# Row projections that close their token tiles over one last weight chunk, and half columns ahead of transposes 2 and 3, in a two-layer decoder trunk

## The reference

```
m = even_mixer(x, w_qkv_ab, w_o_ab, cos, sin)     # layer 0;  odd_mixer(...) in layer 1
x = layer_norm(ALPHA * x + m, ln_mix_g, ln_mix_b)
f = conv_ffn(x, w_up, conv_w, conv_b, w_down)      # (silu(g) * val) @ w_down, g and val convolved
x = layer_norm(ALPHA * x + f, ln_ffn_g, ln_ffn_b)
```

## Time and profile before

| what | us |
|---|---|
| median of 3 runs (1303.65 to 1305.03) | 1305.0 |
| span of the profiled execution | 1303.8 |
| TensorE busy (matmul) | 1251.3 (96%) |
| VectorE busy | 661.0 (51%) |
| GpSimd busy | 558.9 (43%) |
| ScalarE busy | 497.5 (38%) |
| TensorE's mean granted clock over the span, share of full speed | 0.991 |

### The profile page before, as it was taken

One profiled execution on the slowest core, in us unless ns is written; L12 is line 12 of the kernel. 1 busy time (PEld: TensorE's weight loads), 2 busy tenths in 40 slices (PEclk: granted clock), 3 DMA queues, 4 the chain that ended last, 5 costly groups with the idle time before them and its releaser, 6 DMA issues.

```text
span 1303.8 us, 16570 instructions
## 1 busy us (share of the span) xinstructions
PE 1251.3 (96%) x6032; PEld 1022.0 (78%) x6032; DVE 661.0 (51%) x1043; ACT 497.5 (38%) x717; POOL 558.9 (43%) x248
## 2 busy tenths in 40 slices
PE   7999999998999999999989999989899999999996
PEld 7877777688888888888868777768788888888885
DVE  3056656527766666632281255661766666663226
ACT  3234434424433333332242366662443333333222
POOL 4534534323444444445542432332344444444551
PEclk9999999999999999999999999999999999999998
DMA  7221121212222222222213201111222222222211
GB/s 282 97 81 50 64 82 52 78 65 98 97 97 97 97 97 97 97 97 97 97 65 131 97 33 65 64 65 65 98 96 97 95 97 97 96 97 94 98 68 64
DMA packets 19876, 117.22 MB, mean 90 GB/s; under 512 B 2432, under 2 KB 2816, under 8 KB 7424
## 3 DMA queue, kind: packets, MB, share of 16 engines
q1 hardware_dynamic: 18256, 112.21, 23.6%
q10 hardware_dynamic: 1584, 4.51, 1.1%
HBM read 110.41 MB, written 2.10 MB: 86 GB/s over the span
## 4 chain that ended last, share of the span: by engine, by line
PE 52%; issue 26%; POOL 10%; DVE 7%; ACT 4%; DMA 1%; POOLq 0%; SPq 0%; ACTq 0%; DVEq 0%
PE bank L822 27%; PE bank L792 17%; POOL w_lo L215 10%; PE bank L895 3%; PE bank L871 2%; PE bank L881 2%; ACT w_hi L270 2%; DVE probs L667 1%; DVE x L556 1%; ACT probs L342 1%; DVE x L521 1%; PE bank L768 1%; DVE probs L629 1%; DMA x<-x_in 1%; DVE stat L553 0%
## 5 line engine op out<-in xcount | busy, mean ns | idle before, releaser
L215 POOL TENSOR_TENSOR w_lo<-w_raw,w_hi 128x1024 fp32r<-128x1024 f32 x196 | 504.5, 2596 | 632.3 <-ACT w_hi L270 574.6
L822 PE MATMUL bank<-xt_lo,w_hi 128*128 128x512 f32 (+1 forms) x1056 | 403.4, 382 | 0.0
L822 PE MATMUL bank<-xt_hi,w_hi 128*128 128x512 f32 (+1 forms) x1056 | 401.2, 380 | 1.7 <-ACT v_all L307 1.7
L822 PE MATMUL bank<-xt_hi,w_lo 128*128 128x512 f32 (+1 forms) x1056 | 394.8, 374 | 0.0
L270 ACT ACTIVATE w_hi<-w_raw 128x2048 fp32r<-128x2048 f32 x94 | 179.4, 1909 | 206.6 <-PE bank L792 206.6
L822 PEld LDWEIGHTS bank<-xt_lo,w_hi 128*128 128x128 f32 x1056 | 200.2, 190 | 39.3 <-issue 4.8
L822 PEld LDWEIGHTS bank<-xt_hi,w_lo 128*128 128x128 f32 x1056 | 200.0, 189 | 38.3 <-issue 3.7
L822 PEld LDWEIGHTS bank<-xt_hi,w_hi 128*128 128x128 f32 x1056 | 200.3, 190 | 37.8 <-issue 3.1
L792 PE MATMUL bank<-w_hi,a_hi 128*128 128x512 f32 x480 | 153.1, 400 | 2.1 <-POOL w_lo L215 1.2
L792 PE MATMUL bank<-w_lo,a_hi 128*128 128x512 f32 x480 | 150.2, 393 | 0.0
L792 PE MATMUL bank<-w_hi,a_lo 128*128 128x512 f32 x480 | 148.0, 390 | 0.0
(11 more groups left out here) (81 smaller groups left out, 1173.7 us busy)
## 6 DMA issues: line engine op xcount, KB each, us to landing
w_raw<-w_stream SPq DMA_DIRECT2D x97, 1024.0 KB, 4.8
x<-x_in SPq DMA_DIRECT2D x4, 512.0 KB, 7.3
gain<-ln_in ACTq DMA_DIRECT2D x4, 512.0 KB, 4.2
shift<-ln_in ACTq DMA_DIRECT2D x4, 512.0 KB, 5.2
qs<-qc SPq DMA_DIRECT2D x16, 128.0 KB, 2.1
ks<-kc SPq DMA_DIRECT2D x16, 128.0 KB, 2.0
out<-x SPq DMA_DIRECT2D x4, 512.0 KB, 2.6
w_raw<-w_stream SPq DMA_DIRECT2D x2, 512.0 KB, 6.0
```

Of the source, the lines that this page charges most:

```text
L215: pool.tensor_tensor(w_lo[s][:, part], w_raw[s][:, part], w_hi[s][:, part].bitcast(F32), ALU.subtract).then_inc(lo_ready, 1)
L822: mm = pe.matmul(out_bank[:, tok], w, m, start=n == 0, stop=n == len(todo) - 1)
```

## The change

All four tiles close in the last chunk: `last_two` visits the four tiles over the first of the two chunks and then over the second. The transposes of tiles 0 and 1 stand behind the last visit, that of tile 2 behind the first 24 half columns, that of tile 3 behind the next 48 (in the up projection; in layer 1's first stage behind 24 half columns and one visit of the value chunk), and the rest of `meanwhile` behind it. ACT makes `w_hi` of the next stage's first chunk before the norm and in one piece, not in two pieces within it. DVE makes `xt_lo` of tile 0 before the gain multiply of tile 2, and that of tile 1 before the final multiply of tile 2. The second set of `cg`, `cv` and `sig` lies behind a gap in SBUF; `tri` is loaded later and without a wait for the norm. The number of matmuls is the same.

```diff
-            cg = [sb(f"cg{s}", [P, S], stack=st) for s in range(2)]
+            cg, cv, sig = ([sb(f"{n}0", [P, S], stack=st)] for n in ("cg", "cv", "sig"))
+            sb("below_second", [P, S], stack=st)
+            for n, tiles in (("cg", cg), ("cv", cv), ("sig", sig)):
+                tiles.append(sb(f"{n}1", [P, S], stack=st))
...
-                    act.wait_ge(N[1]["xn"], NT)
-                    act.dma_start(tri[:, :], tri_in).then_inc(tri_full, 16)
                     act.wait_ge(a["q_mm"], 1)
...
+                    act.dma_start(tri[:, :], tri_in).then_inc(tri_full, 16)
...
+                heads(b + AT_UP)
                 for i, after in ((2 * l, b + AT_O + 4), (2 * l + 1, b + PER_LAYER)):
...
+                        if l < DEPTH - 1:
+                            heads(after)
...
                         norm_stats(i, 2)
-                        unit_heads(after, 0)
                         xt_heads(i + 1, 1)
-                        unit_heads(after, 1)
                         heads(after + 1)
...
                 norm_sum(i, 2)
+                if turn:
+                    xt_rests(i + 1, 0)
                 norm_mul(i, 2)
                 if turn:
-                    xt_rests(i + 1, 0)
+                    xt_rests(i + 1, 1)
                     norm_out(i, 2)
-                    xt_rests(i + 1, 1)
...
-            last_two = [(0, 0), (1, 0), (0, 1), (1, 1), (2, 0), (2, 1), (3, 0), (3, 1)]
+            last_two = [(t, n) for n in range(2) for t in range(NT)]
...
                     for unit in range(2):
                         for _ in col_unit(c, 0, unit, bank[bank0 + unit], signal, half):
                             pass
+                        if (half, unit) == (0, 0) and i > 0:
+                            turn_x(i, 2)
                     if half == 0 and i > 0:
+                        meanwhile(0)
                         turn_x(i, 3)
-                        meanwhile()
+                        meanwhile(1)
...
                 def first_v(t, _):
+                    if t >= 2:
+                        pe.wait_ge(T[2 * l]["lo"], 2 * t + 2)
...
-                row_steps(out_steps[2:], (a_hi, a_lo), False, True, N[2 * l]["rows"], last_two,
-                          turning(2 * l + 1))
-                turn_x(2 * l + 1, 2)
+                row_steps(out_steps[2:], (a_hi, a_lo), False, True, N[2 * l]["rows"], last_two)
+                turn_x(2 * l + 1, 0)
+                turn_x(2 * l + 1, 1)
...
                 if l < DEPTH - 1:
-                    turn_x(2 * l + 2, 2)
+                    turn_x(2 * l + 2, 0)
+                    turn_x(2 * l + 2, 1)
```

More of the change, by code:

```diff
@@ L52, with slot @@
 STEPS = DEPTH * PER_LAYER
+def slot(c):
+    return c % 2
 EARLY = 12
@@ L214, in rest @@
                     part = slice(u * UNIT, (u + 1) * UNIT)
-                    pool.tensor_tensor(w_lo[s][:, part], w_raw[s][:, part],
-                                       w_hi[s][:, part].bitcast(F32), ALU.subtract).then_inc(lo_ready, 1)
+                    pool.tensor_tensor(w_lo[slot(c)][:, part], w_raw[s][:, part],
+                                       w_hi[slot(c)][:, part].bitcast(F32), ALU.subtract).then_inc(lo_ready, 1)
             def rotate_q(slot, i):
@@ L256, in _ @@
                 rest(b + AT_O + 3)
-                with pool.Fori(0, (PER_LAYER - AT_UP) // 2) as it:
+                rest(b + AT_UP)
+                rest(b + AT_UP + 1)
+                with pool.Fori(0, (PER_LAYER - AT_UP - 2) // 2) as it:
                     for j in range(2):
-                        rest(b + AT_UP + j, it)
+                        rest(b + AT_UP + 2 + j, it)
                 if (PER_LAYER - AT_UP) % 2:
@@ L269, in heads @@
                     act.wait_ge(w_used, c + 2 * it - 1)
[L270 to L277, removed]
+                act.activation(w_hi[slot(c)][:, :], w_raw[c % 2][:, :], ACT.Copy).then_inc(hi_ready, 2)
             def load_gain(i):
@@ L778, in row_tiles @@
                         before(t, m)
-                    c, it, slot = steps[m]
-                    s = c % 2
+                    c, it, at = steps[m]
+                    s = slot(c)
                     opens = m not in [n for _, n in visits[:v]]
@@ L785, in row_tiles @@
                             pe.wait_ge(lo_ready, 2 * (c + 2 * it) + u + 1)
-                        hi = a[0][:, slot + u, t * P:(t + 1) * P]
-                        lo = a[1][:, slot + u, t * P:(t + 1) * P]
+                        hi = a[0][:, at + u, t * P:(t + 1) * P]
+                        lo = a[1][:, at + u, t * P:(t + 1) * P]
                         first = first_chunk and m == 0 and u == 0
@@ L950, in _, with v_meanwhile @@
                                     one_step[1:] + one_step[:1], first_v)
-                def v_meanwhile():
+                def v_meanwhile(_):
                     for _ in range(12):
@@ L997, in up_body, with up_half @@
                         pass
-                def up_half(half):
-                    for unit in range(2):
-                        for _ in col_unit(b + AT_UP + 1, 0, unit, bank[2 + unit], U[l]["g_mm"], half):
-                            pass
-                first_columns(b + AT_UP, 0, U[l]["g_mm"], 2 * l + 1, lambda: up_half(0))
-                up_half(1)
-                with pe.Fori(1, KF // 2) as it:
-                    up_body(0, it)
-                    up_body(1, it)
+                def up_half(half, unit):
+                    for _ in col_unit(b + AT_UP + 1, 0, unit, bank[2 + unit], U[l]["g_mm"], half):
+                        pass
+                first_columns(b + AT_UP, 0, U[l]["g_mm"], 2 * l + 1, lambda unit: up_half(0, unit))
+                up_half(1, 0)
+                up_half(1, 1)
+                with pe.Fori(0, KF // 2 - 1) as it:
+                    up_body(2, it)
+                    up_body(3, it)
                 def down(pairs, first, last):
                     steps = [(b + AT_DN + c, it, 2 * (c % 2)) for c, it in pairs]
-                    turn = turning(2 * l + 2) if last and l < DEPTH - 1 else None
                     def chunk(t, n):
-                        if turn:
-                            turn(t, n)
                         if first and t == 0:
```

2 lines of the change are left out of this document (removed).

## The result

| | kernel before | changed kernel |
|---|---|---|
| median, us | 1305.0 (1303.65 to 1305.05, 4 runs) | 1312.0 (1311.38 to 1313.6, 4 runs) |
| span of the profiled execution | 1303.8 | 1309.6 |
| TensorE busy | 1251.3 | 1250.0 |
| VectorE, GpSimd, ScalarE busy | 661.0, 558.9, 497.5 | 652.6, 562.4, 497.3 |
| mean granted clock | 0.991 | 0.986 |

The changed kernel is slower: the ratio of the times is 1.0058, with a 95% interval of 1.0044 to 1.0072, 7.0 us in the medians and 5.8 in the spans. The forecast was 1309.8, with a range of 1307.0 to 1317.5.

What follows compares the result with a forecast made beforehand. TensorE, busy 96% of 1303.8 us, was taken as the bound, with three waits for x of 13.6 us. Terms 0.9 + 0 + 0.9 + 2.9 = +4.7 gave 1308.5, forecast as median 1309.8, range 1307 to 1317.5.

Steps and rivals of the forecast that it cites:

- Which wait takes the place of the old one: At the boundaries, TensorE's 4.5 us wait for x gives way to 1.5 before transposes 1 and 4.6 before the half columns.
- The near ties of DVE and POOL: At a boundary, two DVE operations and POOL units start nearly together; worth up to 1.7 and 2.1 us each.
- rival (b): At a boundary, POOL's second unit beats multiply 0 and all is 1.7 us later: 1314.9 us; chance 0.12.
- rival (a): At a boundary, POOL beats tile 2's small operation; transposes 2 go 2.1 us later: 1316.2 us; chance 0.28.
- Rival (c): At the boundaries, TensorE restarts at 2.4 GHz and POOL starts after final multiply 2 begins: 1306.0 us; chance 0.11.
- Rival (d): At the boundaries, the waits simply go, 15 us gained: 1290 us; chance 0.04.
- Part 3: Half columns ahead of transposes 2 and 3: +0.9 us at each output projection, 0 at the layer boundary.
- 4.2 if the restart is again at 1.2 GHz for about 3 us: Time for the first 24 half columns after the wait at slow clock, against 2.88 us at 2.4 GHz.
- the mark: Start of the second half of the next stage's first columns; forecast to move from 43.4 to 44.3 us at output projections.
- One value visit more already done, which comes off later: 41.4, so 0: At the layer boundary, the mark at 44.1 less an early value visit of 2.72 us equals the 41.4 of before.
- Part 4: At the kernel's end, DVE's gapless chain over four tiles starts the last final multiply 2.9 us later.
- Part 1: All four tiles close in the last chunk, saving TensorE gaps of 0.28 us, and about 1.2 at the two down projections.

Runs made afterwards that it cites:

- e3: The changed kernel with xt_hi of tile 1 ahead of the statistics of tile 2 and xt_lo of tile 1 ahead of its gain multiply: 1306.7 us.
- e1: The changed kernel with the old order of visits in the last down projection alone: 1309.7 us.
- e5: The changed kernel run once more, nothing altered: 1312.0 us, ratio 1.0052 to the kernel before.
- e2: The kernel before with the new order of visits in the last down projection alone: 1308.7 us.
- e4: The kernel before with DVE's final multiply of tile 2 ahead of the xt_lo of tile 0: 1305.7 us.
- e9: The kernel before with w_hi of the next stage's first chunk behind the xt_hi of tile 1 on ACT: 1307.7 us.
- e7: The kernel before with final multiply of tile 2 ahead of xt_lo 0, and the second chunk's w_hi behind the statistics of tile 3: 1292.9 us.
- e6: The changed kernel with the old visits everywhere and the next first chunk's w_hi behind the statistics of tile 1: 1310.4 us.

## Why the prediction was right, and where it was off

**Which wait takes the place of the old one: right.** It named 1.5 before transposes 1 and 4.6 before the half columns; 1.32 and 4.50 were measured. The half columns start at 29.7 (forecast 29.9), 7.95 after the last visit. e3 shows the cause: with `xt_hi` and `xt_lo` of tile 1 first, 1.74 of the wait goes.

**The near ties of DVE and POOL: the forecast's side, both.** Multiply 0 starts at 15.39 and takes 1.28, ahead of POOL's second unit; rival (b) fell. The last small operation of tile 2 starts at 30.20 and POOL at 30.22; rival (a) fell, by 0.02 us, which is luck and no foresight (though it then falls the same way at all three boundaries, and in e1 and e5 too, where that final multiply takes 3.28 to 3.30 each time). The Trainium skill, "SBUF — State Buffer", Who interferes with whom, calls the port pair that DVE shares with GpSimd an exclusive lock, for which the order of issue decides who blocks: the rows agree, with the operation of 306.39 at 0.16 and the one of 306.58 at 3.29. What the case adds is a duration. DVE gets the port back about 2.2 after a unit's start here, since 306.58 + 3.29 - 1.28 = 308.59, less 306.41.

**Rival (c), not slower: wrong on both its conditions.** TensorE did not restart at 2.4 GHz, and POOL was there before the final multiply. Rival (d), the waits simply go: the order on ACT forbade it, as argued.

**Part 3's sum: the failed term is "4.2 if the restart is again at 1.2 GHz for about 3 us".** The 24 half columns took 5.1 (305.91 to 311.03). I had taken the slow stretch over from the earlier trace rows. In the kernel before it lasts 3.4 (306.65 to 310.05) and begins 0.4 before the transposes, so that TensorE works slowly for 3.0. In the changed kernel it lasts 6.8 (304.0 to 310.8), of which TensorE works 4.9. Transposes 2 then wait for TensorE itself and not for DVE (done at 309.9): 34.8 in place of 34.1 (13.1 after the last visit, not 12.3), and the mark 45.2 in place of 44.3. So +1.8 and +2.0 where +0.9 stood twice.

**"One value visit more already done, which comes off later: 41.4, so 0": half wrong.** The mark there is 0.5 later, by the same long slow stretch. And the visit done early does not come off whole. It stands ahead of the second half columns, so these end 2.9 later (693.65 against 690.76 at their start), the chunk's buffers come free by as much later, and POOL's unit starts at 702.09 for 699.20. But TensorE reaches the second value chunk at nearly the same time as before (704.9 for 704.7), and waits: +0.8. It was a step moved past another queue's release, and I had priced it on TensorE alone.

**Part 4, +2.9: right.** The chain from sum 0 to the last final multiply took 18.14, forecast 18.16; e1 and e2 measured it from both sides.

**Part 1's gain: right in kind.** TensorE has no wait for `w_lo` in the down projections' last chunks any more; e1, which undoes the visits in the last one, has it back.

**The total.** The terms that were named sum to +4.7, the profile's four places to +8.0, the medians to +7.0 and 6.3 (e5). The measured time lies in the range because the rivals had widened it; the forecast's own terms fall short by 3.3, of which 2.0 is mostly the slow stretch at the two output projections and 1.3 the layer boundary. That the dip in the attention varies from one execution to the next may be why the medians show less than 8.0. The fastest executions, which should have the fewest dips, lie 7.7 apart beside each other (1303.65 and 1311.38) and 7.8 in the session of e5 (1303.81 and 1311.56); beyond that it is only argued. No run takes part 3, the half columns ahead of transposes 2 and 3, by itself, so what that part is worth alone is not shown.

## What to carry to other kernels

At the turn from one stage to the next, write down when each engine asks and how long a neighbour holds what it needs, not only TensorE's order: here freeing the one blocked multiply by itself (e4, e9) gained nothing, and moving one weight chunk behind the norm on top of it (e7) gained 12.7 us, about 10 of them at the boundaries. Closing all tiles in the last chunk looks free on TensorE, and takes from the norm the time in which it works beside the last visits. A wait that was seen at one tile is not gone before the next tile's row has been read.

## What the runs showed of the hardware

- The granted clock can fall while TensorE idles, and then the restart pays. In the changed kernel, with 1.3 us and, after eight transposes, 4.5 us of idling the clock was at 0.50 for 6.8 us, 24 half columns taking 5.1; in the kernel before, with one idle stretch of 4.5, it was at 0.50 for 3.4 us. The length of the idling does not tell the two apart: e6, with one idle stretch of 4.7, was at 0.50 for 6.8 us too (305.9 to 312.7). With idle stretches of at most 1.3 at the boundaries (e7) it stayed at 1.00, and the mean over the span is 0.998. So e7's gain is partly the clock's.
- The clock can dip while TensorE is busy: 0.52 for 3.4 us in layer 0's attention, 11 matmuls for 19, in some executions and not in others of the same code. Just before it TensorE had waited twice for `probs`, 1.6 and 1.1 us, and was busy for 1.5 of 3.5 us (2.0 in the changed kernel's profile, where no dip followed). The Trainium skill, "TensorE: Matmul & The Clock Gate", What's actually happening, says that the count of slow matmuls at the start of a kernel differs between runs of the same kernel. The two executions here show such a difference in the middle of one.
- A one-element operation of DVE with two inputs in SBUF is blocked by POOL as a large one is: 2.16 and 2.08 us in e4 for operations that take 0.22 and 0.16 otherwise. With four POOL units in a row, each tile's four small operations can meet a unit more than once.
